# Hybrid attention block on one core: exchanged banks in the first stage, a fourth sum on another engine, probabilities turned a chunk later, values turned sooner

## The chip, the cores and the metric

The kernel runs on one core of a Trainium2 chip. The metric is the device time of one execution in microseconds (us). TensorE (PE in the profile) multiplies, VectorE (DVE), ScalarE (ACT) and GpSimd (POOL) work on elements, and SyncE (SP) issues every DMA. Each engine takes its own instructions strictly in the order written; they meet at semaphores alone.

## The reference

One layer of a streaming encoder on x of 1024 positions by 1024 channels, in fp32. One wide input projection gives queries, keys, values and gates of two mixers:

```
h = x @ w_in + b_in                      # 1024 x 5376 columns
q_a, k_a, v_a, gate_a, q_b, k_b, v_b, gate_b, mg_a, mg_b = split(h)
o_a = window_attention(rope(q_a), rope(k_a), v_a, sinks) * silu(gate_a)   # 16 chunks of 64
o_b = stick_breaking(q_b, k_b, v_b) * silu(gate_b)                        # 128-query blocks
merged = sigmoid(mg_a) * (o_a @ w_up_a) + sigmoid(mg_b) * (o_b @ w_up_b)
out = layer_norm(2**0.25 * x + merged @ w_out)
```

Window attention lets each chunk of 64 queries see its own and one neighbour chunk, with a sink logit in the softmax. Stick breaking multiplies sigmoids along the keys by a running product.

## The kernel before

**Precision.** Every fp32 operand is split into a rounded high part (ScalarE copies it) and a low part (raw minus high, a subtraction on GpSimd or VectorE). A product is three matmuls (`mma3`, lines 176 to 178).

**The projection.** Keys and values of the window mixer (tiles K_A and V_A) are done first and plainly, each in two halves of 512 positions: the keys' halves in PSUM banks 0 and 1, the values' in 2 and 3 (`first_half`). The other 40 column tiles are done as 20 pairs by a seven-product scheme after Strassen, so there are 140 products, numbered q = 7 i + pos. Each is twelve matmuls of 128x512 into bank q % 2. A product needs the low part of its weights (`part_lo`), the bank read out twice earlier (`bank_read`), and in pair 0 also a sum of quarters of x (`t_lo`). There are four sums, t = 1 to 4, made in `xr`, the buffer of raw x: VectorE makes the raw sums 1, 3 and 2 (`sum_raw`), GpSimd the fourth (`fourth_sum`), ScalarE the high parts (`sum_hi`), VectorE the low parts (`sum_lo`). For each pair the second weight tile is loaded by SP (`load_a2`), VectorE forms sums of weights (`weight_sums`), ScalarE and GpSimd split them (`part_high`, `low_part`).

**Rotation.** Rotary positions need halves of each head exchanged. For the keys ScalarE writes them exchanged into `sw` (`keys_swap`), and VectorE then rotates (`rotate_keys`: lines 1072, 1074, 1077). Products 0 and 1 wait for `k_cos` and `swapped`, since they write the banks that the keys stand in. For the queries (pairs 0 and 1) SP exchanges by four DMAs a block (`swap_halves`, line 434), and VectorE rotates (`rotate_block`: lines 1084, 1085, 1088). The first of these exchanges writes `prob`, which lies over `xr`, so SP also waits there for `t_lo` of sums 2 and 4; `load_a2(1)` stands behind it in SP's queue.

**Gates of the window mixer** (pairs 2 and 3) are put in `gate_st`, five slots of which three lie over the angles (`GATE_SLOT`). `room` keeps ScalarE from writing those slots before the queries are rotated.

**The window stage** takes from product 18 on one chunk c with each product: PE turns (transposes) the probabilities of chunk c-2 (line 1457), does the product, the scores of chunk c (line 1471), and the values' product of chunk c-3 (line 1481). VectorE does maxima and norms (lines 1196 to 1221), ScalarE the exponentials (line 924) and the copies of turned probabilities (line 914).

**The sticks**: 16 steps s, each with a big and a small unit of stick breaking between half products (`fill(s, place)`). Banks 6 and 7 serve in turn, in the order of `RING`, for turned weights "t", outputs "o" and turned values "v". Values of the next head pair are turned in steps 4, 8 and 12 (`turn_values`, line 1502; ScalarE copies them in `turned_values`, line 951). A bank may be used when the entry two back is read out: for the second half of the values that is the output of the small unit of the step before, which VectorE reads in `gated_out` (line 1258, semaphore `o_set`) only after the big unit's scans and multiplications:

```
for s in range(STEPS):
    break_sticks(s, False)
    if s > 0:
        gated_out(s - 1, True)
```

Of the kernel before, what the change touches and what calls it, by code (L numbers as in the profile page):

```python
# [51 lines left out]
BLOCKS = ((0, 0), (0, 1), (1, 1), (1, 0))  # L52
GATE_SLOT = {(0, 0): 0, (0, 1): 2, (1, 1): 4, (1, 0): 1}

# [126 lines left out]
def build(nc, xt, xn, w, bias, cos, sin, sinks, ln_g, ln_b, out):  # L181
    with ExitStack() as ctx:
# [42 lines left out]
        with ExitStack() as a1:  # L225
            qa23 = sb("qa23", [P, NCHUNK, 2, CHUNK], F32, a1)
            v_win = sb("v_win", [P, NCHUNK, P], F32, a1)
            prob = sb("prob", [P, 3, HALF], F32, a1)
            prob_t = sb("prob_t", [P, 2, HALF], F32, a1)
            oa_st = sb("oa_st", [P, 2, GROUP, P], F32, a1)  # L230
            gate_st = sb("gate_st", [P, 5, HALF], F32, a1)
        qa = (qa01, qa23)
# [92 lines left out]
        def block_at(sp, m, nh):  # L325


            if sp in Q_PAIRS:
                return qa[sp][:, 8 * nh:8 * nh + 8, m, :]
            if sp in G_PAIRS:  # L330
                return gate_st[:, GATE_SLOT[m, nh], :]
            if sp >= MG_PAIR:
                return sig_m[:, 4 * (sp % 2) + 2 * m + nh, :]
            for p in range(PAIRS):
                if sp == pair_vg(p):
                    return (o_b[p % 2] if m else v_t)[:, half(nh)]
                if sp == pair_kq(p):
                    return (qs if m else ks)[p % 2][:, half(nh)]
# [30 lines left out]
        oa_done, oa_free, oa_out = sem("oa_done"), sem("oa_free"), [sem(f"oa_out{i}") for i in range(2)]  # L369
        gate_out = [sem(f"gate_out{i}") for i in range(5)]  # L370
        z_done, keep_set, beta_set = sem("z_done"), sem("keep_set"), sem("beta_set")
# [30 lines left out]

        window_end = WINDOW_1 + NCHUNK + 2

        @block.sync
        def _(sp):
# [30 lines left out]
            def gate_store(i, m, nh):  # L437
                wait_block(sp, i, m, nh)
                at = GATE_SLOT[m, nh]
                sp.dma_start(gate_d[2 * (i - G_PAIRS[0]) + m][:, half(nh)],  # L440
                             gate_st[:, at, :]).then_inc(gate_out[at], 16)

# [79 lines left out]
            for q in range(WINDOW_1):  # L522
                after(q)
            for c in range(NCHUNK + 3):
                if c < NCHUNK + 2:
                    after(WINDOW_1 + c)
                if c >= 4 and c % 2 == 0:
                    window_store((c - 4) // 2)
            for q in range(window_end, STEP_0):
# [70 lines left out]
        def _(pool):  # L600
# [17 lines left out]

            def fourth_sum(i):


                if i == 0:
                    pool.wait_ge(x_lo_done, 2 * KT)
                pool.wait_ge(t_raw[2], i + 1)
                o = x_raw(1, 0, i)
                pool.tensor_tensor(o, o, x_raw(1, 1, i), ALU.subtract).then_inc(t_raw[4], 1)

            def cut_causal(s, small):
# [45 lines left out]
        def _(act):  # L674
# [33 lines left out]
            def keys_swap(h):  # L708


                act.wait_ge(half_done, halves_done(K_A, h))
                for q in range(4):
                    o = 32 * (q ^ 1)
                    act.activation(sw[o:o + 32, h, :], ps[32 * q:32 * q + 32, h, :], ACT.Identity,
                                   bias=b_of(K_A, 32 * q, 32 * q + 32)).then_inc(swapped, 1)

            def value_half(h):
                act.wait_ge(half_done, halves_done(V_A, h))
                act.activation(v_t[:, half(h)], ps[:, 2 + h, :], ACT.Identity, bias=b_of(V_A)).then_inc(v_read, 1)

# [16 lines left out]
            def room(i, pos):  # L737
# [6 lines left out]
                if i == G_PAIRS[0]:  # L744
                    if pos == 0:
                        act.wait_ge(t_lo[2], 2)
                    else:
                        act.wait_ge(rope_done, rope_at(Q_PAIRS[1], 3 if pos == 6 else 2) + 1)
                if i == G_PAIRS[1]:
                    act.wait_ge(gate_out[GATE_SLOT[m, nh]], 16)  # L750
                for p in range(PAIRS):
                    if i == pair_kq(p) and pos == 0:
                        if p == 0:
                            act.wait_ge(rope_done, rope_at(Q_PAIRS[1], 3) + 1)
                            act.wait_ge(gate_out[GATE_SLOT[1, 1]], 16 * len(G_PAIRS))
# [149 lines left out]
            act.wait_ge(t_lo[4], 2)  # L905
            for c in range(NCHUNK + 2):
                if c >= 2:
                    i = c - 2
                    rows = P if i < NCHUNK - 1 else CHUNK
# [33 lines left out]
            def turned_values(p):  # L943

                if p == 1:
                    for m in range(2):
                        act.wait_ge(gate_out[GATE_SLOT[m, 1 - m]], 16 * len(G_PAIRS))
                for g in range(2):
# [23 lines left out]
            for s in range(STEPS):  # L972
# [10 lines left out]
                if s % 4 == 0 and s > 0:  # L983
                    gate_b_sigmoid(s // 4)
                for q in completed(s, 2):
                    read_bank(q)
                if s % 4 == 0 and s > 0:
                    turned_values(s // 4)
                turned_blocks(s, False, (0, 1))
# [50 lines left out]
        def _(dve):  # L1040
# [5 lines left out]
            def sum_raw(t):  # L1046


                for i in range(2):
# [4 lines left out]
                    elif t == 3:  # L1054
                        dve.wait_ge(t_raw[1], i + 1)
                        dve.tensor_tensor(o, x_raw(1, 1, i), o, ALU.subtract).then_inc(t_raw[t], 1)
                    else:
                        dve.wait_ge(t_raw[3], i + 1)
                        dve.tensor_tensor(o, o, x_raw(0, 0, i), ALU.subtract).then_inc(t_raw[t], 1)

            def sum_lo(t):
# [7 lines left out]
            def rotate_keys(h):  # L1069
                k_ = ka[:, half(h)]  # L1070
                dve.wait_ge(swapped, 4 * (h + 1))
                dve.scalar_tensor_tensor(out=k_, in0=ps[:, h, :], scalar=bias_c[:, K_A:K_A + 1],
                                         in1=cos_t[:, half(h)], op0=ALU.add, op1=ALU.mult).then_inc(k_cos, 1)
# [105 lines left out]
            sum_raw(2)  # L1179
            dve.wait_ge(rope_in, 32)  # L1180
            rotate_keys(0)
            weight_sums(0, True)
            sum_lo(2)
            weight_sums(0, False)
            rotate_keys(1)
            sum_lo(3)
            sum_lo(1)
            sum_lo(4)
            for q in range(WINDOW_1):
                after(q)  # L1190
# [13 lines left out]
            dve.wait_ge(sink_set, 1)  # L1204
            for c in range(NCHUNK + 3):
                if 1 <= c <= NCHUNK:
                    prob_norm(c - 1)
                if c < NCHUNK:
# [12 lines left out]
                    dve.tensor_tensor(sm[:, 1, 0:4], sm[:, 0, 0:4], sink_c[:], ALU.add).then_inc(za_bias, 1)  # L1221
                if c < NCHUNK + 2:
# [143 lines left out]
        def _(pe):  # L1366
# [4 lines left out]
            def first_half(n, h):  # L1371


                bank = 2 + h if n == V_A else h
                for k in range(KT):
# [16 lines left out]
            def half_product(u):  # L1392
# [56 lines left out]

            for c in range(NCHUNK + 3):  # L1450
                if 2 <= c < NCHUNK + 2:
                    i = c - 2
                    keys = P if i < NCHUNK - 1 else CHUNK
# [5 lines left out]
                    last.then_inc(tp_done, 1)  # L1459
                if c < NCHUNK + 2:  # L1460
                    product(WINDOW_1 + c)
                if c < NCHUNK:
# [10 lines left out]
                    last.then_inc(za_done, 1)  # L1473
                if c >= 3:
                    i = c - 3
                    pe.wait_ge(tp_free, 4 + i + 1)
# [88 lines left out]
            for s in range(STEPS):  # L1565
# [161 lines left out]
```

## Time and profile before

| | |
|---|---|
| Median of three runs | 773.39 us (772.83, 773.39, 777.02) |
| Profiled execution | 776.86 us |
| Its span, first to last instruction | 775.1 us |
| Mean granted TensorE clock | 0.99 |
| Busy: PE, DVE, ACT, POOL | 742.1, 528.4, 404.6, 251.7 us |

The span is what the trace shows; 1.8 us of the profiled execution lie outside it. Spans of matmuls overlap, so the spacing of their starts says more than their length. "[7.26 <-issue]" behind a row is the idle time ahead of it and what ended it; "issue" means that the trace names no releaser.

### The profile page before, as it was taken

What the parts mean: (1) busy time and instruction counts of PE and PEld (TensorE: products, weight loads), DVE (VectorE), ACT (ScalarE), POOL (GpSimd) and SP (SyncE); (2) the same over time, 40 slices, a digit from 0 to 9 for tenths busy, and PEclk for the clock granted to TensorE, in tenths of its full rate; (3) what the DMA queues carried; (4) which work ended last, traced back from release to release, by engine and by line L of the source; (5) the groups of instructions that cost most, each with busy time, mean ns of one, the idle gap of its engine ahead of it and who ended that gap; (6) DMA issues with size and microseconds to landing.
All of it is one profiled execution on the core that took longest, in us unless ns stands there. A gap on an engine that the chain in (4) does not pass through costs nothing.

```text
span 775.1 us, 10717 instructions
## 1 busy us (share of the span) xinstructions
PE 742.1 (96%) x3944; PEld 580.3 (75%) x3944; DVE 528.4 (68%) x684; ACT 404.6 (52%) x760; POOL 251.7 (32%) x225
## 2 busy tenths in 40 slices
PE   8789889999999999999999999999999999999996
PEld 7567666766677777777777777888887888888884
DVE  6987887883579768786977876344457566770644
ACT  6833356664766567676657765555565121150221
POOL 0544423223332123223212323445443221200692
PEclk9989999999999999999999999999999999999998
DMA  9114432222010020102001222355554444341351
GB/s 312 69 34 103 91 100 82 84 67 69 28 55 29 28 82 1 55 1 82 28 28 59 79 69 69 125 183 194 189 193 132 178 164 158 114 164 54 114 199 68
DMA packets 41204, 76.22 MB, mean 98 GB/s; under 512 B 12224, under 2 KB 16320, under 8 KB 41152
## 3 DMA queue, kind: packets, MB, share of 16 engines
q1 hardware_dynamic: 41152, 75.54, 29.9%
q8 instruction: 32, 0.52, 0.3%
q14 instruction: 20, 0.16, 0.1%
HBM read 55.07 MB, written 18.35 MB: 95 GB/s over the span
## 4 chain that ended last, share of the span: by engine, by line
PE 69%; DVE 16%; ACT 5%; DMA 3%; issue 3%; SPq 2%; POOL 1%; ACTq 0%; DVEq 0%; POOLq 0%
PE ps L176 19%; PE ps L178 18%; PE ps L177 18%; PE ps L1519 5%; PE ps L1548 5%; PE ps L1535 4%; DVE small L1218 2%; ACT prob L924 2%; DMA raw<-in_w 2%; DVE prob L1201 1%; DVE small L1214 1%; DVE t_ops L1066 1%; SPq L434 1%; DMA xr<-in_xt 1%; DVE raw L1108 1%
## 5 line engine op out<-in xcount | busy, mean ns | idle before, releaser
L176 PE MATMUL ps<-x_hi,w_hi 128*128 128x512 f32 x448 | 182.9, 408 | 8.8 <-issue 7.3
L178 PE MATMUL ps<-x_hi,w_lo 128*128 128x512 f32 x448 | 175.9, 393 | 0.0
L177 PE MATMUL ps<-x_lo,w_hi 128*128 128x512 f32 x448 | 175.5, 392 | 0.0
L616 POOL TENSOR_TENSOR w_lo<-raw,w_hi 128x512 fp32r<-128x512 f32 x72 | 100.9, 1412 | 100.2 <-ACT w_hi L706 100.0
L176 PE MATMUL ps<-t_ops,w_hi 128*128 128x512 f32 x272 | 110.3, 406 | 5.8 <-ACT gate_st L798 4.0
L176 PEld LDWEIGHTS ps<-x_hi,w_hi 128*128 128x128 f32 x448 | 84.7, 189 | 36.1 <-issue 14.9
L178 PE MATMUL ps<-t_ops,w_lo 128*128 128x512 f32 x272 | 107.0, 393 | 0.0
L177 PE MATMUL ps<-t_ops,w_hi 128*128 128x512 f32 x272 | 106.8, 393 | 0.0
L178 PEld LDWEIGHTS ps<-x_hi,w_lo 128*128 128x128 f32 x448 | 84.6, 189 | 18.3
L177 PEld LDWEIGHTS ps<-x_lo,w_hi 128*128 128x128 f32 x448 | 84.9, 190 | 15.3
L1241 DVE TENSOR_TENSOR_SCAN keep_big<-keep_big 128x1023 f32<-128x1023 f32 (+3 forms) x32 | 63.4, 1981 | 31.1 <-POOL keep_big L636 29.1
L706 ACT ACTIVATE w_hi<-raw 128x512 fp32r<-128x512 f32 x120 | 73.5, 632 | 6.7 <-DVE raw L1114 3.4
L636 POOL TENSOR_SCALAR_AFFINE_SELECT keep_big<-keep_big 128x128 f32<-128x128 f32 x32 | 29.5, 923 | 139.6 <-ACT keep_big L963 139.6
L176 PEld LDWEIGHTS ps<-t_ops,w_hi 128*128 128x128 f32 x272 | 51.5, 189 | 21.3 <-issue 8.9
L178 PEld LDWEIGHTS ps<-t_ops,w_lo 128*128 128x128 f32 x272 | 51.5, 189 | 11.3
L177 PEld LDWEIGHTS ps<-t_ops,w_hi 128*128 128x128 f32 x272 | 51.5, 189 | 9.7
L793 ACT ACTIVATE tmp<-ps 128x512 f32<-128x512 f32 x60 | 36.1, 601 | 42.1 <-PE ps L178 42.1
L1099 DVE TENSOR_TENSOR sig_m<-sig_m,tmp 128x512 f32<-128x512 f32 x32 | 24.4, 784 | 40.5 <-ACT tmp L793 40.5
L963 ACT ACTIVATE keep_big<-ps 128x1023 f32<-128x1023 f32 (+3 forms) x32 | 25.9, 862 | 38.9 <-PE ps L1519 38.9
L1519 PE MATMUL ps<-ks,qs 64*128 64x512 f32 (+3 forms) x192 | 39.6, 517 | 0.9 <-ACT beta_big L965 0.9
L1332 DVE SCALAR_TENSOR_TENSOR o_t<-raw,ps 128x512 f32<-128x512 f32 x16 | 10.9, 683 | 43.0 <-PE ps L178 34.6
L1121 DVE TENSOR_TENSOR w_lo<-raw,w_hi 128x512 fp32r<-128x512 f32 x48 | 34.7, 738 | 8.0 <-ACT w_hi L706 8.0
(170 smaller groups left out, 1311.3 us busy)
## 6 DMA issues: line engine op xcount, KB each, us to landing
raw<-in_w SPq DMA_DIRECT2D x28, 512.0 KB, 3.9
raw<-in_w SPq DMA_DIRECT2D x44, 256.0 KB, 3.0
sig_d<-sig_m SPq DMA_DIRECT2D x32, 256.0 KB, 3.3
sig_m<-sig_d SPq DMA_DIRECT2D x16, 512.0 KB, 4.2
xr<-in_xt SPq DMA_DIRECT2D x16, 256.0 KB, 6.8
raw<-in_xn SPq DMA_DIRECT2D x8, 512.0 KB, 3.7
out<-o_t SPq DMA_DIRECT2D x16, 256.0 KB, 2.3
o_t<-o_d SPq DMA_DIRECT2D x7, 512.0 KB, 4.9
```

What stands on the lines that cost most here:

```text
L176: pe.matmul(out, w_hi, x_hi, start=first, stop=False, skip_group_check=goes_on)
L177: pe.matmul(out, w_hi, x_lo, start=False, stop=False, skip_group_check=goes_on)
L178: return pe.matmul(out, w_lo, x_hi, start=False, stop=last, skip_group_check=goes_on)
L616: pool.tensor_tensor(ring_slot(w_lo, q), part_of(q), ring_slot(w_hi, q).bitcast(F32), ALU.subtract).then_inc(part_lo, 1)
L636: pool.affine_select(out=kp_d, in_=kp_d, compare_op=ALU.is_gt, fill=1.0, base=0, pattern=[[1, n]], channel_multiplier=-1).then_inc(keep_cu ...
L706: act.activation(ring_slot(w_hi, q), part_of(q), ACT.Copy).then_inc(part_hi, 1)
L793: act.activation(tmp[:, e % 2, :], bank, ACT.Copy).then_inc(bank_read, 1)
L1121: dve.tensor_tensor(ring_slot(w_lo, q), part_of(q), ring_slot(w_hi, q).bitcast(F32), ALU.subtract).then_inc(part_lo, 1)
L1241: dve.tensor_tensor_scan(stick, stick, stick, 1.0, ALU.mult, ALU.bypass).then_inc(scanned, 1)
L1519: last = pe.matmul(ps[:, 2 + 2 * h + at // HALF, 0:m], qs[p % 2][r, P * tb:P * (tb + 1)], ks[p % 2][r, P * tb + at:P * tb + at + m], start ...
L1535: last = pe.transpose(bank[:, at:at + P], bt[:, h, P * b_:P * (b_ + 1)], ident[:])
L1548: last = pe.matmul(bank[r, 0:P], v_n[p % 2][:, tb + b_, r], w_t[:, turned_block(small, b_), h, :], start=b_ == 0, stop=b_ == nb - 1)
```

## The change

Six edits:

1. Keys and values exchange banks: values in 0 and 1, keys in 2 and 3. Products 0 and 1 now wait for ScalarE's copies of the values (`v_read`).
2. The fourth sum goes from GpSimd to VectorE, behind the other three.
3. VectorE rotates the keys only after all sums but behind the first addition of a block (`after(0)`, `after(1)`).
4. `gate_st` has two slots; blocks (0,1) and (1,1) go to `sw`. ScalarE waits there for the keys' rotation instead of the queries'.
5. PE turns the probabilities of chunk c-3 instead of c-2, and everything behind it in the chunk loop comes one chunk later.
6. `turn_values` on PE stands ahead of `fill(s, 2)`, and `turned_values` on ScalarE ahead of `read_bank` of that place.

```diff
-GATE_SLOT = {(0, 0): 0, (0, 1): 2, (1, 1): 4, (1, 0): 1}
+GATE_SLOT = {(0, 0): 0, (1, 0): 1, (0, 1): 2, (1, 1): 3}
...
-                return gate_st[:, GATE_SLOT[m, nh], :]
+                slot = GATE_SLOT[m, nh]
+                return gate_st[:, slot, :] if slot < 2 else sw[:, slot - 2, :]
...
-            fourth_sum(0)
-            low_part(0)
-            low_part(1)
-            fourth_sum(1)
-            low_part(2)
+            for q in range(3):
+                low_part(q)
...
+                    elif pos == 6:
+                        act.wait_ge(rope_done, rope_at(Q_PAIRS[1], 3) + 1)
                     else:
-                        act.wait_ge(rope_done, rope_at(Q_PAIRS[1], 3 if pos == 6 else 2) + 1)
+                        act.wait_ge(rope_done, 2)
...
+            value_half(0)
             keys_swap(0)
-            value_half(0)
             sum_hi(1)
             sum_hi(3)
             part_high(0)
             part_high(1)
             sum_hi(2)
             keys_swap(1)
+            value_half(1)
             part_high(2)
-            value_half(1)
             sum_hi(4)
...
                     if q < 2:
-                        pe.wait_ge(k_cos, q + 1)
-                        pe.wait_ge(swapped, 4 * (q + 1))
+                        pe.wait_ge(v_read, q + 1)
...
-            for c in range(NCHUNK + 3):
-                if 2 <= c < NCHUNK + 2:
-                    i = c - 2
+            for c in range(NCHUNK + 4):
+                if 3 <= c < NCHUNK + 3:
+                    i = c - 3
...
-                if c >= 3:
-                    i = c - 3
+                if c >= 4:
+                    i = c - 4
...
                 scores(s, True)
-                fill(s, 2)
                 if s % 4 == 0 and s > 0:
                     turn_values(s // 4)
+                fill(s, 2)
                 turn(s, False, (0, 1))
```

**VectorE, from the fourth raw sum to the first exchange of a block of queries.** xr is raw x and its sums, t_ops and x_lo take the low parts, raw and w_x are weights, ka and sw the keys, qa the queries; in brackets stand the semaphores waited for. Before:

```order
L1072 SCALAR_TENSOR_TENSOR ka<-ps,bias_c,angles 128x512 [waits swapped,rope_in]
L1074 TENSOR_TENSOR sw<-sw,angles 128x512
L1077 TENSOR_TENSOR ka<-ka,sw 128x512 [waits sin_mul,k_cos]
L1108 TENSOR_TENSOR raw<-raw 128x512 [waits part_lo,a2_in]
L1110 TENSOR_TENSOR w_x<-raw 128x512 [waits w_sum]
L1066 TENSOR_TENSOR t_ops<-xr,t_ops 128x1024 [waits t_hi2] x2
L1114 TENSOR_TENSOR raw<-raw,w_x 128x512 [waits w_sum,part_lo]
L1115 TENSOR_TENSOR raw<-raw 128x512
L1072 SCALAR_TENSOR_TENSOR ka<-ps,bias_c,angles 128x512 [waits swapped]
...
L1066 TENSOR_TENSOR x_lo<-xr,x_hi 128x2x512 [waits t_hi4] x2
L1099 TENSOR_TENSOR qa<-qa,tmp 128x8x64 [waits bank_read] x2
```

Of the change (its line numbers are a few lower):

```order
L1052 TENSOR_TENSOR xr<-xr 128x2x512 [waits t_raw2] x2
L1101 TENSOR_TENSOR raw<-raw 128x512 [waits part_lo,a2_in]
L1103 TENSOR_TENSOR w_x<-raw 128x512 [waits w_sum]
L1059 TENSOR_TENSOR t_ops<-xr,t_ops 128x1024 [waits t_hi2] x2
L1107 TENSOR_TENSOR raw<-raw,w_x 128x512 [waits w_sum,part_lo]
L1108 TENSOR_TENSOR raw<-raw 128x512
L1059 TENSOR_TENSOR t_ops<-xr,t_ops 128x1024 [waits t_hi3] x2
L1059 TENSOR_TENSOR t_ops<-xr,t_ops 128x1024 [waits t_hi1] x2
L1092 TENSOR_TENSOR qa<-qa,tmp 128x8x64 [waits bank_read]
L1059 TENSOR_TENSOR x_lo<-xr,x_hi 128x2x512 [waits t_hi4] x2
L1065 SCALAR_TENSOR_TENSOR ka<-ps,bias_c,angles 128x512 [waits swapped,rope_in]
```

The six operations of the keys have moved behind the low part of the fourth sum (x_lo), and two operations of the fourth raw sum have come in ahead.

**PE, in step 4 of the sticks, from the small unit's scores to the turning of the big unit's weights.** ks and qs are keys and queries, v_t the values to be turned, beta_big the weights. Before:

```order
L1519 MATMUL ps<-ks,qs 128x128 [waits beta_set]
...
L176 MATMUL ps<-t_ops,w_hi 128x512 [waits bank_read,part_lo]
...
L1502 MATMUL ps<-ident,v_t 128x128 [waits turned_out,block_sum]
L1502 MATMUL ps<-ident,v_t 128x128 x3
L1502 MATMUL ps<-ident,v_t 128x128 [waits o_set]
L1502 MATMUL ps<-ident,v_t 128x128 x3
L1535 MATMUL ps<-ident,beta_big 128x128 [waits turned_out,w_ready]
```

Of the change:

```order
L1515 MATMUL ps<-ks,qs 128x128 [waits beta_set]
L1515 MATMUL ps<-ks,qs 128x128
L1498 MATMUL ps<-ident,v_t 128x128 [waits turned_out,block_sum]
L1498 MATMUL ps<-ident,v_t 128x128 x3
L1498 MATMUL ps<-ident,v_t 128x128 [waits o_set]
L1498 MATMUL ps<-ident,v_t 128x128 x3
L176 MATMUL ps<-x_hi,w_hi 128x512
...
L1531 MATMUL ps<-ident,beta_big 128x128 [waits turned_out,w_ready]
```

The eight transposes now stand ahead of the twelve matmuls of two half products, and the wait for `o_set` with them.

## Rows read from the trace of the kernel before

**Rows 1.** The page, part 1: TensorE's busy time, share of the span, instructions.

```profile
PE 742.1 (96%) x3944; PEld 580.3 (75%) x3944; DVE 528.4 (68%) x684; ACT 404.6 (52%) x760; POOL 251.7 (32%) x225
```

**Rows 2.** Waits of PE: us in total, times, longest.

```profile
PE ps L176 <- issue: 7.3, 1, 7.3
PE ps L1457 <- DVE prob L1201: 4.9, 8, 1.6
PE ps L176 <- ACT gate_st L798: 4.0, 1, 4.0
...
PE ps L1535 <- ACT v_n L951: 1.1, 3, 0.4
```

**Rows 3.** Timeline of PE, products 0 and 1: start us, us, what.

```profile
31.65 0.50 PE L176 MATMUL ps<-x_hi,w_hi 128*128 128x512 f32 x1 [0.46 <-POOL w_lo L616]
...
34.27 0.39 PE L178 MATMUL ps<-x_hi,w_lo 128*128 128x512 f32 x1
41.92 0.77 PE L176 MATMUL ps<-x_hi,w_hi 128*128 128x512 f32 x1 [7.26 <-issue]
```

**Rows 4.** Windows, 42 to 45 us: busy of each engine, then PEclk, DMA.

```profile
42.00:45.00 3.00, 3.00 (x7) 2.40 (x8) 2.90 (x3) 0.00 (x0) 2.26 (x2) 0.50 0.30 87
```

**Rows 5.** Timeline of DVE, 27 to 56 us.

```profile
27.54 0.74 DVE L1072 SCALAR_TENSOR_TENSOR ka<-ps,bias_c,angles 128x512 f32<-128x512 f32 x1
...
44.73 4.62 DVE L1066 TENSOR_TENSOR t_ops<-xr,t_ops 128x1024 fp32r<-128x1024 f32 x4
49.27 4.55 DVE L1066 TENSOR_TENSOR x_lo<-xr,x_hi 128x1024 fp32r<-128x1024 f32 x2
53.74 2.40 DVE L1099 TENSOR_TENSOR qa<-qa,tmp 128x512 f32<-128x512 f32 x2
```

**Rows 6.** Timeline of POOL, the same stretch.

```profile
26.64 3.26 POOL L626 TENSOR_TENSOR xr<-xr 128x1024 f32<-128x1024 f32 x1 [25.11 <-DVE xr L1059]
...
48.22 2.27 POOL L616 TENSOR_TENSOR w_lo<-raw,w_hi 128x512 fp32r<-128x512 f32 x1 [3.97 <-ACT w_hi L706]
```

**Rows 7.** Timeline of ACT: the keys' second exchange.

```profile
30.26 2.80 ACT L714 ACTIVATE sw<-ps,bias_c 32x512 f32<-32x512 f32 x4
```

**Rows 8.** Timeline of SP: the first exchange of queries, the weights behind it.

```profile
55.56 2.70 SPq L434 DMA_DIRECT2D prob<-qa  x4
58.30 0.60 SPq L420 DMA_DIRECT2D raw<-in_w  x1
```

**Rows 9.** Timelines of DVE and PE: who needs those weights.

```profile
63.32 0.69 DVE L1108 TENSOR_TENSOR raw<-raw 128x512 f32<-128x512 f32 x1 [1.40 <-DMA raw<-in_w]
```

```profile
67.12 0.50 PE L176 MATMUL ps<-t_ops,w_hi 128*128 128x512 f32 x1 [0.62 <-POOL w_lo L616]
```

**Rows 10.** Timelines of PE and DVE ahead of the window stage.

```profile
97.40 0.60 PE L176 MATMUL ps<-t_ops,w_hi 128*128 128x512 f32 x1 [3.99 <-ACT gate_st L798]
...
101.91 0.72 PE L1471 MATMUL ps<-ka,qa 64*128 64x128 f32 x8
```

```profile
98.39 1.59 DVE L1088 TENSOR_TENSOR qa<-qa,prob_t 128x512 f32<-128x512 f32 x1
```

**Rows 11.** Timelines of ACT and PE in the window stage.

```profile
121.38 0.61 ACT L914 ACTIVATE prob_t<-ps 128x512 f32<-128x512 f32 x1
```

```profile
122.69 0.65 PE L1457 MATMUL ps<-ident,prob 128*128 128x128 f32 x4 [1.23 <-DVE prob L1201]
...
179.23 0.65 PE L1481 MATMUL ps<-prob_t,v_win 128*64 128x256 f32 x4 [0.18 <-DVE oa_st L1229]
```

**Rows 12.** Timeline of PE and DVE in step 4 of the sticks.

```profile
277.84 0.50 PE L176 MATMUL ps<-x_hi,w_hi 128*128 128x512 f32 x1
...
279.85 0.28 DVE L1258 TENSOR_TENSOR o_b<-o_b,ps 128x128 f32<-128x128 f32 x1
...
280.75 1.04 PE L1502 MATMUL ps<-ident,v_t 128*128 128x128 f32 x8
...
282.21 1.12 PE L1535 MATMUL ps<-ident,beta_big 128*128 128x128 f32 x8 [0.42 <-ACT v_n L951]
```

More of the change, by code:

```diff
@@ L369, in build @@
         oa_done, oa_free, oa_out = sem("oa_done"), sem("oa_free"), [sem(f"oa_out{i}") for i in range(2)]
-        gate_out = [sem(f"gate_out{i}") for i in range(5)]
+        gate_out = [sem(f"gate_out{i}") for i in range(4)]
         z_done, keep_set, beta_set = sem("z_done"), sem("keep_set"), sem("beta_set")
@@ L400, in rope_at @@
             return 2 + 4 * i + b
-        window_end = WINDOW_1 + NCHUNK + 2
+        window_end = WINDOW_1 + NCHUNK + 3
         @block.sync
@@ L523, in _ @@
                 after(q)
-            for c in range(NCHUNK + 3):
-                if c < NCHUNK + 2:
+            for c in range(NCHUNK + 4):
+                if c < NCHUNK + 3:
                     after(WINDOW_1 + c)
-                if c >= 4 and c % 2 == 0:
-                    window_store((c - 4) // 2)
+                if c >= 5 and c % 2 == 1:
+                    window_store((c - 5) // 2)
             for q in range(window_end, STEP_0):
@@ L718, in value_half @@
                 act.wait_ge(half_done, halves_done(V_A, h))
-                act.activation(v_t[:, half(h)], ps[:, 2 + h, :], ACT.Identity, bias=b_of(V_A)).then_inc(v_read, 1)
+                act.activation(v_t[:, half(h)], ps[:, h, :], ACT.Identity, bias=b_of(V_A)).then_inc(v_read, 1)
             def first_weights_hi(n, h):
@@ L754, in room @@
                             act.wait_ge(rope_done, rope_at(Q_PAIRS[1], 3) + 1)
-                            act.wait_ge(gate_out[GATE_SLOT[1, 1]], 16 * len(G_PAIRS))
+                            for m in range(2):
+                                act.wait_ge(gate_out[GATE_SLOT[m, 1]], 16 * len(G_PAIRS))
                         else:
@@ L905, in _ @@
             act.wait_ge(t_lo[4], 2)
-            for c in range(NCHUNK + 2):
-                if c >= 2:
-                    i = c - 2
+            for c in range(NCHUNK + 3):
+                if c >= 3:
+                    i = c - 3
                     rows = P if i < NCHUNK - 1 else CHUNK
@@ L945, in turned_values @@
                 if p == 1:
-                    for m in range(2):
-                        act.wait_ge(gate_out[GATE_SLOT[m, 1 - m]], 16 * len(G_PAIRS))
+                    act.wait_ge(gate_out[GATE_SLOT[1, 0]], 16 * len(G_PAIRS))
                 for g in range(2):
@@ L984, in _ @@
                     gate_b_sigmoid(s // 4)
+                    turned_values(s // 4)
                 for q in completed(s, 2):
                     read_bank(q)
-                if s % 4 == 0 and s > 0:
-                    turned_values(s // 4)
                 turned_blocks(s, False, (0, 1))
@@ L1179, in _ @@
             sum_raw(2)
-            dve.wait_ge(rope_in, 32)
-            rotate_keys(0)
+            sum_raw(4)
             weight_sums(0, True)
@@ L1184, in _ @@
             weight_sums(0, False)
-            rotate_keys(1)
             sum_lo(3)
             sum_lo(1)
+            after(0)
+            after(1)
             sum_lo(4)
-            for q in range(WINDOW_1):
+            dve.wait_ge(rope_in, 32)
+            rotate_keys(0)
+            after(2)
+            rotate_keys(1)
+            for q in range(3, WINDOW_1):
                 after(q)
@@ L1204, in _ @@
             dve.wait_ge(sink_set, 1)
-            for c in range(NCHUNK + 3):
+            for c in range(NCHUNK + 4):
                 if 1 <= c <= NCHUNK:
@@ L1371, in first_half @@
             def first_half(n, h):
-                bank = 2 + h if n == V_A else h
+                bank = 2 + h if n == K_A else h
                 for k in range(KT):
@@ L1448, in _ @@
                     last.then_inc(tp_done, 1)
-            for c in range(NCHUNK + 3):
-                if 2 <= c < NCHUNK + 2:
-                    i = c - 2
+            for c in range(NCHUNK + 4):
+                if 3 <= c < NCHUNK + 3:
+                    i = c - 3
                     keys = P if i < NCHUNK - 1 else CHUNK
@@ L1459, in _ @@
                     last.then_inc(tp_done, 1)
-                if c < NCHUNK + 2:
+                if c < NCHUNK + 3:
                     product(WINDOW_1 + c)
@@ L1473, in _ @@
                     last.then_inc(za_done, 1)
-                if c >= 3:
-                    i = c - 3
+                if c >= 4:
+                    i = c - 4
                     pe.wait_ge(tp_free, 4 + i + 1)
```

21 lines of the change are left out of this document (9 added, 12 removed).

## The prediction

> **What bounds the kernel now.** I read the page first: TensorE is busy 742.1 of 775.1 us [rows 1], so whatever delays it counts in full, and the question is where it idles. The list of its waits gives four entries that the change aims at: 7.3 us once, 4.0 us once, 4.9 us in eight pieces at the turning of probabilities, 1.1 us in three at the turning of values [rows 2]. Then I read the timeline of each place.
>
> The 7.3 us lie between product 0, whose last matmul starts at 34.27, and product 1 at 41.92 [rows 3]. The trace says "issue", but product 1 waits for `k_cos`, whose second operation (line 1072) ends on VectorE when PE starts. The row 42 to 45 us has a granted clock of 0.50, the 1.2 GHz level [rows 4]; the first ten matmuls start 0.43 us apart instead of 0.23, which is 2.0 us more. So the place costs up to 0.5 + 7.3 + 2.0 = 9.8 us. The 3.99 us ahead of 97.40 [rows 10] are ScalarE kept in `room` until the queries are rotated; nine matmuls at the low clock follow, 1.8 us.
>
> What limits the stretch between them? Not PE. The chain of waits runs there through SP, the DMAs and VectorE: four exchange DMAs from 55.56, the weights behind them in SP's queue at 58.30 [rows 8], landed for VectorE at 63.32, and through ScalarE and GpSimd to PE at 67.12, which had idled 0.62 us for it [rows 9]. It goes on in that way to the last rotation, which ends at 98.39 + 1.59 = 99.98; the scores of chunk 0 at 101.91 need it [rows 10].
>
> **Edits 1 to 3, the head.** PE itself: values replace keys in ScalarE's list. Its first copy waits for the values' half, so the list runs some 0.35 us later; the keys' second exchange, 30.26 + 2.80 before [rows 7], ends at 33.4, the second copy of values at 34.1. Product 1 starts there instead of 41.92: 7.8 us, and without the slow clock. But product 6 needs the low part of the fourth sum, and, what matters more, SP needs it before the exchange at 55.56. I therefore sum VectorE's list.
>
> Prices first. Four operations on 1024 elements take 4.62 us, 1.14 each, while GpSimd rests; two of the same kind take 4.55 when GpSimd has two subtractions beside them (one is the 2.27 us row at 48.22) [rows 5, 6]. So each of GpSimd's operations costs VectorE 1.14 us: they exclude each other. Of the two additions in 2.40 us one such piece leaves 0.62 for an operation on 512 elements [rows 5].
>
> The Trainium skill, page "SBUF — State Buffer", section "SBUF: two separate sides", says the same of a VectorE operation with two SBUF inputs against a GpSimd operation that reads SBUF: an exclusive lock for the whole instruction, not shared bandwidth. If they did not exclude each other the list below would be 10 us shorter; this case's rows side with the page.
>
> The new list starts where line 1072 started, 27.54 [rows 5]: two of the fourth sum, eight low parts (ten at 1.14 = 11.4), four weight sums and one addition (five at 0.62 = 3.1), 14.5 us together. GpSimd now has nothing but low parts of weights in that time, and since PE runs earlier they come sooner: parts 0 to 8 are all ready before the end (part 8 after product 4, which ends near 46), in turn with VectorE, nine by 1.14 = 10.3 us. `t_lo` of sum 4 is complete at 27.5 + 14.5 + 10.3 = 52.3. Before, SP's exchange was released by the first addition at 55.5. The advance is 3.2 us; with ten of GpSimd's in it 2.1, with seven 5.5.
>
> All that follows on SP, DMA and VectorE keeps its distances: exchange at 52.4, weights issued at 55.1, product 9 able to start at 67.12 - 3.2 = 63.9. PE would be there near 59.8 (product 6 waits until 52.5 for the fourth sum, ends at 53.9; two products at 2.73, four transposes). So a wait of about 4 us takes the place of the one of 7.3. The keys' rotation, moved behind, takes some 4 us from 52.3 and lies under the DMAs, which end at 56.6 and 60.1; without that cover it would stand in the chain.
>
> **Edit 4, the gates.** The 3.99 us and the 1.8 us of slow clock disappear at that place. But the scores of chunk 0 wait for the same rotation, one product later. It now ends at 99.98 - 3.2 = 96.8. PE, with a slow clock after the gap at product 9, gets there near 95.0 and waits 2 us; without the slow clock it waits 4. Either way the scores start at 96.85 against 101.91: **5.1 us gained** by edits 1 to 4 together, of which 1.9 is PE's former lateness against the rotation. Bounds: 2.1 + 1.9 = 4.0 and 5.5 + 1.9 = 7.4.
>
> **Edit 5, probabilities a chunk later.** It looks like 4.9 us. But from 107 to 175 the chain of waits runs through VectorE and ScalarE alone: norm, maximum, bias, four exponentials, norm again, which takes 4.3 to 5.9 us a chunk, while PE's own work for one is 4.63 where it waits for nothing (transposes at 116.83, the next ones could go at 121.46; the rows of this stretch of the timeline are too many to stand here). Those operations don't move. With one chunk more between, PE's transposes are no longer bound by the norm, but by the bank: ScalarE copies the turned probabilities of c-4 only behind the exponentials of c-2. That copy starts at 121.38 and ends at 121.99, where the norm let PE go at 122.69 [rows 11]. PE runs 0.6 us closer to the loop, once, not per chunk. At the end it waits for the copy of an output by VectorE (0.18 us at 179.23 [rows 11]), which stays where it is. I take **0.3 us gained**, between 0.6 and a loss of 1.0 (if PE, which is ahead by a chunk at first and then waits some 2.5 us in one piece, falls to the low clock there, or at the scores).
>
> **Edit 6, values sooner.** This loses. In step 4 PE starts the two half products at 277.84, the values at 280.75, and the big unit's weights at 282.21, after 0.42 us for ScalarE's copy [rows 12]. Moved ahead, the first four transposes can run at 277.84, but the second four wait for `o_set`, and VectorE reads that output at 279.85 to 280.13 [rows 12], behind scans and multiplications that hang on the big unit's scores, already past. So PE idles from 278.36 to 280.18, turns to 280.70, does its half products (2.91 us, 277.84 to 280.75) until 283.61, and only then the weights: 1.4 us later than before, the 0.42 included. The half products were the cover of that wait. Steps 8 and 12 have the same rows 68.5 and 136.9 us later; **4.2 us lost** in all, 3.7 to 4.7. PE has hardly a wait left in those steps that could absorb it.
>
> **Sum.** -5.1 - 0.3 + 4.2 = -1.2 us: the profiled 776.86 becomes 775.7, the span 773.9. The profiled execution lies 3.5 us above the median of the three runs, so I take the difference from the median: 773.39 - 1.2 = **772.2 us**. The likeliest case's own range is 773.39 - 7.4 - 0.6 + 3.7 = 769.1 to 773.39 - 4.0 + 1.0 + 4.7 = 775.1. A measurement of this kernel tells about 0.5%, 3.9 us, from no change: one of the three runs is 3.6 above the others.
>
> **The rivals.**
> (a) The chain through SP is no limit, and PE's own earliness survives (chance 0.10). It needs VectorE's list to end by about 46, so hardly any exclusion. PE would reach product 9 at 59.8, 7.3 us early, and with 3.99 + 1.8 more at the gates gain 13.1: 773.39 - 13.1 - 0.3 + 4.2 = 764.2. Against it speak rows 5 and 6.
> (b) The values' move costs nothing and removes its 1.1 us (0.08): if VectorE read the output before PE asks. 773.39 - 5.1 - 0.3 - 1.1 = 766.9. Against it: 279.85 lies 1.5 us behind the point at which PE would ask [rows 12].
> (c) Slower than before: VectorE's list is not earlier (0.12). It carries the fourth sum and nine subtractions in turn; if the exclusion costs more, or SP's exchange is released at 55.5 as before, only the 1.9 us remain: 773.39 - 1.9 + 4.2 = 775.7. The point from which it decides is an end of the list at 53.5: there the gain of the head equals edit 6.
> (d) The clock. The Trainium skill, page "TensorE: Matmul & The Clock Gate", section "HAM oscillation — how this bites in real kernels", says that gaps in the matmuls bring the clock back to its low level each time; rows show it after 7.26 and 3.99 us of idleness [rows 3, 4, 10] and not after 1.23 [rows 11]. The change makes gaps of about 4 us ahead of product 9, 2 ahead of the scores and 2.5 in the window stage. Only one behind the scores would count, about 2 us: 774.2 (0.10).
>
> The rest, 0.60, is the forecast. From these: faster than before by over 0.5% 0.28 ((a), (b) and a tenth of the forecast's lower edge with the scatter of runs), within 0.5% 0.62, slower 0.10. The range has to hold (b) and (c) with the scatter: 766.8 to 776.8.
>
> **What would show it.** Right: in the changed trace PE starts product 1 near 34; SP's first exchange is issued near 52.4; PE waits some 4 us for GpSimd's part ahead of product 9 near 64; the scores start near 97; the turning of probabilities waits for ScalarE's copy; in steps 4, 8 and 12 PE idles 1.8 us ahead of the second half of the values, for line 1258's successor. Wrong: an exchange issued before 48 or after 55, no wait ahead of product 9, a chunk of the window stage in under 4.7 us, or no wait in the middle of the values.

## The result, and the profile after

The change takes 778.28 us (median of 20 runs, 774.52 to 780.73), the kernel before, run beside it, 775.15 us (20 runs, 772.22 to 777.60). The ratio is 1.0049, 95% interval 1.0037 to 1.0061: 3.8 us slower by the ratio, 3.1 by the two medians. The interval leaves out 1, so the change is slower, though just inside the 0.5% that the forecast called no change. Forecast were 1.2 us faster, and 778.28 lies above the range's 776.8. Ratios here and below leave out runs far off the others of their kernel: one of e9's nine, at 919.33 us, and one of the 21 of before beside e9 to e11, at 2107.13 us.

The profiled execution of the change took 776.80 us, 1.5 us less than its median. That of before took 776.86 us, 1.7 us more than its median. By these two the change looks like -0.06 us.

The page of the changed kernel, first part:

```profile
PE 740.8 (96%) x3944; PEld 578.8 (75%) x3944; DVE 528.1 (68%) x686; ACT 404.9 (52%) x760; POOL 251.1 (32%) x223
```

TensorE's work is the same [rows 1]. Its list of waits (us in total, times, longest):

```profile
PE ps L1498 <- DVE o_b L1255: 5.0, 3, 1.7
PE ps L176 <- POOL w_lo L617: 4.5, 1, 4.5
PE ps L1453 <- ACT prob_t L906: 3.7, 5, 1.5
PE ps L1477 <- DVE oa_st L1226: 2.8, 5, 1.3
PE ps L1467 <- DVE qa L1081: 2.4, 1, 2.4
PE ps L176 <- DVE x_lo L1059: 1.6, 2, 1.1
```

Against [rows 2] the 7.3 and the 4.0 us are gone, but 4.5 wait for a weight's low part, 2.4 for the last rotation, 1.6 for the fourth sum. The turning of probabilities now waits for ScalarE's copy. And 5.0 us in three pieces are new: the turning of values in steps 4, 8 and 12.

The head, timeline of PE:

```profile
33.81 0.47 PE L176 MATMUL ps<-x_hi,w_hi 128*128 128x512 f32 x1 [0.37 <-ACT v_t L708]
...
49.38 0.47 PE L176 MATMUL ps<-x_hi,w_hi 128*128 128x512 f32 x1 [1.11 <-DVE x_lo L1059]
...
51.51 0.50 PE L176 MATMUL ps<-x_hi,w_hi 128*128 128x512 f32 x1 [0.53 <-DVE x_lo L1059]
...
63.58 0.80 PE L176 MATMUL ps<-t_ops,w_hi 128*128 128x512 f32 x1 [4.53 <-POOL w_lo L617]
...
97.49 0.71 PE L1467 MATMUL ps<-ka,qa 64*128 64x128 f32 x8 [2.39 <-DVE qa L1081]
```

Timelines of DVE, POOL and SP in the same stretch:

```profile
37.39 7.91 DVE L1059 TENSOR_TENSOR t_ops<-xr,t_ops 128x1024 fp32r<-128x1024 f32 x4
45.22 1.78 DVE L1092 TENSOR_TENSOR qa<-qa,tmp 128x512 f32<-128x512 f32 x1
46.93 4.53 DVE L1059 TENSOR_TENSOR x_lo<-xr,x_hi 128x1024 fp32r<-128x1024 f32 x2
51.38 0.74 DVE L1065 SCALAR_TENSOR_TENSOR ka<-ps,bias_c,angles 128x512 f32<-128x512 f32 x1
```

```profile
37.61 12.77 POOL L617 TENSOR_TENSOR w_lo<-raw,w_hi 128x512 fp32r<-128x512 f32 x6 [1.29 <-ACT w_hi L695]
```

```profile
51.56 2.70 SPq L435 DMA_DIRECT2D prob<-qa  x4
54.31 0.60 SPq L421 DMA_DIRECT2D raw<-in_w  x1
```

The prediction's chain can be read off here. Product 1 starts at 33.81. VectorE's list ends at 51.46, SP's exchange goes out at 51.56, product 9 starts at 63.58 after 4.53 us of idleness, the scores at 97.49 (101.91 in [rows 10]). From 37.39 on VectorE's and GpSimd's operations go in turn: VectorE's four take 7.91 us where they took 4.62 [rows 5], GpSimd's six take 2.1 each. Behind the 4.53 us the granted clock is 0.50 from 64 to 69 us; that costs nothing, since PE then still waits 2.39 us for the scores' rotation.

Step 4, timelines of PE and DVE:

```profile
273.73 0.49 PE L1515 MATMUL ps<-ks,qs 64*128 64x128 f32 x4
274.15 0.66 PE L1498 MATMUL ps<-ident,v_t 128*128 128x128 f32 x4
276.48 0.66 PE L1498 MATMUL ps<-ident,v_t 128*128 128x128 f32 x4 [1.67 <-DVE o_b L1255]
276.89 0.47 PE L176 MATMUL ps<-x_hi,w_hi 128*128 128x512 f32 x1
...
279.74 1.03 PE L1531 MATMUL ps<-ident,beta_big 128*128 128x128 f32 x8
```

```profile
276.15 0.27 DVE L1255 TENSOR_TENSOR o_b<-o_b,ps 128x128 f32<-128x128 f32 x1
```

PE turns the first four blocks at 274.15 and then stands 1.67 us until VectorE has read the output. From the first four blocks to the big unit's weights it is 5.59 us here; in [rows 12], from the half products that stood there (277.84) to the weights (282.21), 4.37. So 1.22 us are lost at each of three places.

Lastly the stretches. From the first values' turning behind the window stage to the end of the span it is 581.8 us before (775.1 - 193.34) and 585.5 in the change (775.1 - 189.65): 3.7 us, all of it edit 6 (e1 below, which differs in edit 6 alone, has 581.8 again). Between scores and values lie 91.43 us before and 92.16 in the change: 0.7 lost where edit 5 was to gain.

### The profile page after: what moved, and what is told of

The parts are those of the page before. It is cut to its first block, busy times and chain, and to the rows that moved or that the text cites. A ratio compares the mean times of both kernels' runs of the same rounds, so it can differ in the third digit from the quotient of the medians.

```text
span 775.1 us, 10717 instructions
## 1 busy us (share of the span) xinstructions
PE 740.8 (96%) x3944; PEld 578.8 (75%) x3944; DVE 528.1 (68%) x686; ACT 404.9 (52%) x760; POOL 251.1 (32%) x223
## 4 chain that ended last, share of the span: by engine, by line
PE 69%; DVE 17%; ACT 5%; issue 4%; DMA 3%; POOL 2%; SPq 1%; DVEq 0%; ACTq 0%; POOLq 0%
PE ps L176 19%; PE ps L178 18%; PE ps L177 18%; PE ps L1515 5%; PE ps L1544 4%; PE ps L1531 4%; ACT prob L916 2%; DVE small L1215 2%; DMA prob<-qa 1%; DVE prob L1198 1%; DVE keep_big L1238 1%; DVE small L1211 1%; DMA raw<-in_w 1%; DVE beta_big L1245 1%; DVE qa L1078 1%
## 5 line engine op out<-in xcount | busy, mean ns | idle before, releaser
L617 POOL TENSOR_TENSOR w_lo<-raw,w_hi 128x512 fp32r<-128x512 f32 x72 | 104.3, 1462 | 118.8 <-ACT w_hi L695 118.7
L617 POOL TENSOR_TENSOR w_lo<-w_x,w_hi 128x512 fp32r<-128x512 f32 x12 | 17.5, 1458 | 75.5 <-ACT w_hi L695 75.5
```

Source lines behind the costliest of these rows:

```text
L617: pool.tensor_tensor(ring_slot(w_lo, q), part_of(q), ring_slot(w_hi, q).bitcast(F32), ALU.subtract).then_inc(part_lo, 1)
```

## The experiments

The first four ask which part carries the loss, and how much of the difference belongs to the execution that was traced. The next four price the edits: 1 to 4 together, then 5 alone, 4 alone, and 1 to 3, which were not separated further. The last four test the cause in edit 6 and look for a better version. "Before" is always the kernel before, run beside the experiment on the same chip.

**e1: the change without edit 6.**

```
                 betas(s, True)
                 if s % 4 == 0 and s > 0:
                     gate_b_sigmoid(s // 4)
-                    turned_values(s // 4)
                 for q in completed(s, 2):
                     read_bank(q)
+                if s % 4 == 0 and s > 0:
+                    turned_values(s // 4)
...
                 scores(s, True)
+                fill(s, 2)
                 if s % 4 == 0 and s > 0:
                     turn_values(s // 4)
-                fill(s, 2)
```

> The change without edit 6 (values turned where they were before). Theory: edit 6 costs 3.6 us, 1.2 us at each of three places, so this kernel is 3.6 us faster than the change and within 1.5 us of the kernel before. Rival (the loss lies in the head or the window stage): it stays 3 to 4 us slower than before.

Measured: 773.31 us (12 runs), ratio 0.9978 [0.9965, 0.9992]; the stretch from values to the end is back at 581.8 us. Against the change's 1.0049 edit 6 costs 0.7%, some 5.5 us. The place is right, but the waits explain only 3.7 of it.

**e2: before with edit 6** (the same lines in the kernel before).

> The kernel before with edit 6 alone. Theory: 3.6 us slower than before, ratio 1.0047, with PE idle 1.7 us ahead of the second half of the values in steps 4, 8 and 12. Rival: under 1.5 us slower.

Measured: 779.14 us (7 runs), 1.0068 [1.0039, 1.0098]. So 5.3 us by the ratio, without any of the other edits. Its windows (us, busy of PE, PEld, DVE, ACT and POOL, PEclk, DMA) from 338 and from 405, over the turnings of steps 8 and 12:

```profile
338.00:355.00 17.00, 15.08 (x85) 11.22 (x84) 13.68 (x17) 10.13 (x18) 5.07 (x6) 0.90 0.19 63
405.00:425.00 20.00, 18.08 (x119) 13.56 (x119) 17.71 (x22) 12.80 (x23) 5.07 (x6) 1.00 0.14 43
```

The granted clock fell at step 8, not at step 12. This was the first sign of what the waits leave unexplained.

**e3 and e4: before and the change once more, unedited.**

> The kernel before once more, for a second trace. If the profiled execution of before (1.7 us above the median) was an odd one, this trace shows a shorter span, and where: the theory is a low clock or none after the 4 us gap ahead of product 18, 1.8 us. Ratio to before 1.000.

> The changed kernel once more, for a second trace. Its profiled execution was 1.5 us below its median at the highest clock of all its runs (0.994 against 0.989 to 0.991). Theory: a usual execution has one more stretch at the low clock, after a gap that the change made (product 6, product 9, the scores, or the window stage), worth 1.5 to 2 us. Ratio to before 1.0049.

Measured: before again 775.25 us, 0.9998 [0.9980, 1.0017], and its trace has the gap of 4.0 us of [rows 10] and the low clock behind it again. The first profile of before was therefore no odd one at this place. Its span is 774.1 us, 1.0 less, all of it ahead of the scores (100.89 against 101.91). The change again: 778.87 us, 1.0055 [1.0036, 1.0075], and its trace differs from the change's first, timeline of PE at the scores and at step 8:

```profile
96.33 0.94 PE L1467 MATMUL ps<-ka,qa 64*128 64x128 f32 x8 [3.60 <-DVE qa L1081]
97.20 0.79 PE L176 MATMUL ps<-t_ops,w_hi 128*128 128x512 f32 x1
97.80 0.63 PE L177 MATMUL ps<-t_ops,w_hi 128*128 128x512 f32 x1
...
343.25 0.65 PE L1498 MATMUL ps<-ident,v_t 128*128 128x128 f32 x4
345.58 0.89 PE L1498 MATMUL ps<-ident,v_t 128*128 128x128 f32 x4 [1.68 <-DVE o_b L1255]
346.12 0.77 PE L176 MATMUL ps<-x_hi,w_hi 128*128 128x512 f32 x1
346.70 0.63 PE L177 MATMUL ps<-x_lo,w_hi 128*128 128x512 f32 x1
...
350.44 1.03 PE L1531 MATMUL ps<-ident,beta_big 128*128 128x128 f32 x8
```

Here PE waits 2.83 us ahead of product 9, not 4.53, and 3.60 at the scores, not 2.39. And the big unit's weights come 7.19 us after the first four blocks, where step 4 of the change's first trace has 5.59: 1.6 us more, with the same wait of 1.7. The expectation had the low clock among four places, of which the scores were one; steps 8 and 12 were not among them. Matmuls take 0.63 us instead of 0.40, the level of 1.2 GHz. The windows of this trace, as above:

```profile
338.00:355.00 17.00, 15.08 (x88) 11.98 (x86) 12.38 (x14) 11.85 (x22) 4.77 (x5) 0.90 0.20 63
405.00:425.00 20.00, 18.08 (x111) 13.73 (x107) 15.05 (x19) 12.91 (x23) 5.07 (x6) 0.91 0.16 53
```

The change's first trace has 1.00 in both:

```profile
338.00:355.00 17.00, 15.09 (x109) 12.21 (x109) 13.08 (x15) 12.47 (x22) 5.06 (x6) 1.00 0.19 63
405.00:425.00 20.00, 18.09 (x126) 13.95 (x124) 14.59 (x19) 14.04 (x24) 5.07 (x6) 1.00 0.18 53
```

The stretch to the end follows: 585.5 us with none of these drops (first trace), 587.0 with one (e2), 588.6 with two (e4), some 1.6 us each.

**e5: edits 1 to 4** (the change without edits 5 and 6: the lines of e1 and these, with the loops of the engines one chunk shorter).

```
-                if c >= 3:
-                    i = c - 3
+                if c >= 2:
+                    i = c - 2
```

> Edits 1 to 4 alone (5 and 6 undone). Theory: edit 5 costs 0.9 us in the window stage (92.2 to 92.8 us from the first scores to the first values, against 91.4), so this kernel is 2.6 us faster than before (ratio 0.9966), and the stretch takes 91.4 us again. Rival, as forecast: edit 5 gains 0.3 us, so this kernel is no faster than the one with edit 5 (ratio 0.998 or above).

Measured: 771.83 us (770.70 to 772.84), 0.9968 [0.9954, 0.9983], 2.5 us faster. Its span of 770.3 is 4.8 us under the 775.1 of before's first trace, close to the 5.1 forecast against that execution. Both numbers are true: before's runs beside it (35) lie in three groups, around 772.4, 774.1 and 776.0 us, and both traces of before come from the upper one; e5's runs have one group.

**e6: before with edit 5.**

> The kernel before with edit 5 alone. Theory: the window stage is bound by VectorE and ScalarE, the waits of PE move from the norm to ScalarE's copy and to VectorE's copy of outputs; 0.9 us slower, ratio 1.001, stretch of 92.3 us. Rival by the list of waits: 4.9 us faster.

Measured: 776.07 us, 1.0020 [1.0002, 1.0038]: 1.5 us slower. Its waits in the window stage:

```profile
PE ps L1457 <- ACT prob_t L914: 4.1, 5, 1.9
...
PE ps L1481 <- DVE oa_st L1229: 2.8, 5, 1.3
```

The 4.9 us that the norm cost have become 4.1 for the bank, and the wait for VectorE's copies of outputs has grown from 0.8 to 2.8 us: 1.2 us more together; from scores to values it takes 92.48 us (91.43 before). The rival, 4.9 us gained, has fallen.

**e7: before with edit 4.**

```
-GATE_SLOT = {(0, 0): 0, (0, 1): 2, (1, 1): 4, (1, 0): 1}
+GATE_SLOT = {(0, 0): 0, (1, 0): 1, (0, 1): 2, (1, 1): 3}
...
+                    elif pos == 6:
+                        act.wait_ge(rope_done, rope_at(Q_PAIRS[1], 3) + 1)
                     else:
-                        act.wait_ge(rope_done, rope_at(Q_PAIRS[1], 3 if pos == 6 else 2) + 1)
+                        act.wait_ge(rope_done, 2)
```

> The kernel before with edit 4 alone (gates in the swap buffer). Theory: the 4.0 us wait for the gates moves one product on, to the scores of chunk 0, which start 1.9 us earlier than before at the end of the rotation; a low clock behind the gap takes about 1 us of it back: 0.5 to 1.9 us faster. Rival by the list of waits: 5.8 us faster (4.0 and 1.8 of low clock).

Measured: 774.08 us, 0.9989 [0.9974, 1.0003]. The 4.0 us ahead of 97.40 are gone, and 3.25 of them stand a product later, timeline of PE:

```profile
98.68 1.23 PE L1474 MATMUL ps<-ka,qa 64*128 64x128 f32 x8 [3.25 <-DVE qa L1091]
99.84 0.79 PE L176 MATMUL ps<-t_ops,w_hi 128*128 128x512 f32 x1
```

The low clock has moved with the wait. The rival, 5.8 us gained, has fallen.

**e8: before with edits 1 to 3** (the diff's parts on banks, the fourth sum and VectorE's list).

> Edits 1 to 3 alone (banks, fourth sum, keys rotated later; gates as before). Theory: the chain from the low part of the fourth sum through SP and the DMAs is 3 to 4 us earlier, and the wait for the gates, which ends with the same rotation, moves with it: product 18 starts at 93 to 94.5 instead of 97.4, the result is 2.5 to 3.5 us faster. Rival (PE's own earliness survives): 8 us or more.

Measured: 772.09 us, 0.9975 [0.9958, 0.9992], 1.9 us faster, less than the 2.5 to 3.5 expected; the scores start at 96.72. PE waits 4.6 us ahead of product 9. Its runs lie in two groups, around 771.5 and 773.7 us. Product 18 starts at 93.79, after 1.9 us for the gates, as expected. The rival, eight or more for the 7.3 us taken away, has fallen. With e7's 0.9989 this makes 0.9964, e5's 0.9968 within the scatter.

**e9: edits 1 to 4, and only the first half of the values ahead.** Four blocks are turned ahead of `fill(s, 2)`, which covers the wait, and four behind it; ScalarE's two copies in `turned_values` are parted in the same way. Shown against e5:

```
                 scores(s, True)
+                if s % 4 == 0 and s > 0:
+                    turn_values(s // 4, (0,))
                 fill(s, 2)
                 if s % 4 == 0 and s > 0:
-                    turn_values(s // 4)
+                    turn_values(s // 4, (1,))
```

> Edits 1 to 4, and of the values only the first half turned sooner (ahead of the half products), the second half where it was. Theory: the loss of edit 6 is the wait of the second half for the output bank; without it the first half's copy is hidden and the waits of 0.42 us shrink: 0 to 1 us faster than edits 1 to 4 alone, ratio to before 0.996. Rival (the transposes' early place itself costs, or splits the clock): slower than edits 1 to 4.

Measured: 771.46 us, 0.9954 [0.9933, 0.9976]. No wait for `o_b` is left in its trace, timeline of PE:

```profile
273.41 0.66 PE L1500 MATMUL ps<-ident,v_t 128*128 128x128 f32 x4
...
276.66 0.60 PE L1500 MATMUL ps<-ident,v_t 128*128 128x128 f32 x4
```

So it was the loss of the cover that cost, not the early turning itself: against the change's 1.0049 both the wait and edit 5 are gone, against e5's 0.9968 nothing is lost. That it beats e5 isn't shown: the intervals overlap.

**e10: edits 1 to 4, the next weights sent ahead of the exchange** and their sum formed between the two rotations of keys.

```
-                if pos == 2 and i + 1 < N_PAIRS:
+                if pos == (1 if i == 0 else 2) and i + 1 < N_PAIRS:
...
+            weight_sums(1, True)
```

> Edits 1 to 4, with the second weights of pair 1 loaded ahead of the first exchange in SP's queue and summed between the two rotations of keys. Theory: the wait of 3 to 4.5 us ahead of product 9 goes, since it hangs on SP's order alone; but the scores still wait for the rotation, which comes only 1.2 us earlier, and PE's wait moves there (5 us and more, with a low clock behind it): 0 to 1.5 us faster than edits 1 to 4. Rival (PE's earliness is worth itself): 3 us or more faster than edits 1 to 4.

Measured: 770.89 us, 0.9950 [0.9929, 0.9971]. The waits, which were 4.2 and 2.5 in e5, are

```profile
PE ps L1469 <- DVE qa L1082: 3.9, 1, 3.9
...
PE ps L176 <- POOL w_lo L617: 2.4, 1, 2.4
```

Of what product 9 no longer waits (1.8 us) the scores wait 1.4: they hang on the last rotation. They start 1.5 us sooner (96.17 against 97.69), but a low clock follows the longer wait and takes that back: from scores to values it takes 92.43 us against 90.97 in e5.

**e11: the change, with its idle stretch filled.** Twelve transposes of the unit matrix, which nobody reads, stand ahead of the second four blocks.

```
                 for g in range(2):
+                    if g and p:
+                        for _ in range(12):
+                            pe.transpose(ps[:, 5, 0:P], ident[:], ident[:])
```

> The whole change with 12 transposes of the identity in an unused bank ahead of the second half of the values in steps 4, 8 and 12, in the 1.7 us in which PE idles. They compute nothing that is used. Theory: of the 5.3 us that edit 6 costs, 3.65 are its wait and the rest is the low clock that follows the idle stretch in some executions; with the stretch filled the granted clock is 1.00 at all three places in the profile and the ratio falls from 1.005 to 1.0025. Rival (the clock has no part in it): 1.005 or more.

Measured: 776.93 us (774.50 to 777.88), 1.0025 [1.0008, 1.0043], and step 4 in its timeline of PE:

```profile
274.95 0.66 PE L1501 MATMUL ps<-ident,v_t 128*128 128x128 f32 x4
275.44 1.47 PE L1498 MATMUL ps<-ident 128*128 128x128 f32 x12
277.28 0.66 PE L1501 MATMUL ps<-ident,v_t 128*128 128x128 f32 x4 [0.37 <-DVE o_b L1255]
```

The second four blocks come 2.33 us after the first, as in the change: nothing is gained in the wait. The clock is 1.00 over steps 4, 8 and 12 in its trace, and the ratio is 0.0024 under the change's in the first comparison (0.0030 under e4's): 1.9 to 2.3 us. Useless work made the kernel faster, as far as this can be told: the intervals of e11 and of the change just overlap (1.0043 and 1.0037), so the size is loose. Against e1, the same kernel without edit 6, e11 is still 0.0047 or 3.6 us slower, with intervals well apart: the price of the three waits alone, three times 1.22 us.

**e12: e9 and e10 together.**

> Edits 1 to 4 with both: the weights ahead of the exchange, and the first half of the values sooner. Theory: the two gains add, 1.4 and 1.1 us over edits 1 to 4 alone, ratio to before 0.994 (0.992 to 0.996). Rival: no better than either alone, 0.995.

Measured: 771.37 us (7 runs, 770.10 to 771.59), before 775.39, 0.9943 [0.9921, 0.9965], the lowest ratio of all. It beats before and the change; that it beats e5, e9 or e10 isn't shown.

## Why the prediction was wrong, step by step

Measured are 778.28 us, 6.1 above the forecast 772.2. Of these 1.8 are the base: the forecast started from 773.39, the median of three runs, where 20 give 775.15; from that base the same range would have ended at 778.6 and held the result. The rest is the change itself, forecast 1.2 us faster and measured 3.8 slower by the ratio, and there three steps of the sum failed: a difference within one trace was taken off the median (edits 1 to 4, 5.1 forecast, 2.5 measured), edit 5 had the wrong sign (0.3 gained against 0.8 to 1.5 lost), and edit 6 was priced by its wait alone (4.2 against 5.5).

**Edits 1 to 3, the head: right.** "`t_lo` of sum 4 is complete at … 52.3" (measured 51.46), "exchange at 52.4" (51.56), "product 9 able to start at … 63.9" (63.58), "a wait of about 4 us takes the place of the one of 7.3" (4.53). The reading that the 7.3 us hid a chain through VectorE, SP and the DMAs held; rival (a) has fallen with the 4.53 us, rival (c) with the exchange at 51.56. One assumption, that all behind the exchange "keeps its distances", holds only roughly: from SP's exchange to product 9 pass 12.0 us in the change's first trace, 10.3 in its second (51.88 to 62.20) and 11.6 before. The mutual exclusion of VectorE and GpSimd, on which the list's length hung, shows in both engines' rows.

**Edit 4: right.** The scores started at 97.49 and 96.33 in two traces, forecast 96.85; e7 shows that the wait only moves to "the same rotation, one product later". By the ratio e7 gains 0.9 us, and its interval holds 1, so a gain of edit 4 alone isn't shown.

**The difference from one trace, taken off the median: this step failed, and it is the largest miss (2.6 us).** The forecast took a difference worked out in one execution, "5.1 us gained", off the median of the runs. Between traces it is 4.8 us (e5), but by the ratio only 2.5. Before's runs form groups, and against the lowest (772.4) edits 1 to 4 gain next to nothing, against the upper one (776.0), from which the trace came, 4.2. What differs inside before between the groups wasn't traced, since both traces come from the upper one, and stays open. Their mean clocks are about 0.993, 0.988 and 0.990, so it isn't the clock alone.

**Edit 5: wrong sign.** "PE runs 0.6 us closer to the loop" held at the bank, but "At the end it waits for the copy of an output by VectorE …, which stays where it is" failed. The outputs are made a chunk later, too, and the wait for their copies grew from 0.8 to 2.8 us. They are five waits instead of two, the first already at 139.78 us and not at the stage's end; why VectorE comes to these copies late wasn't followed. Measured: 1.5 us lost (e6, interval 0.2 to 2.9), and 0.8 us between e5 and e1 (0.9968 and 0.9978, whose intervals overlap), forecast 0.3 gained. It lies at or just beyond the loss of 1.0 that was kept as a bound.

**Edit 6: mechanism right, price too small.** PE idles ahead of the second four blocks in exactly the three places, 1.67 us for a forecast 1.8, and loses 1.22 us at each for a forecast 1.4: 3.7 for 4.2. But it costs 5.3 to 5.5 us (e2; e1 against the change). The step that failed stands under rival (d): "Only one behind the scores would count". In the head that held: the low clock behind product 9 cost nothing. But the prediction looked for low clocks behind gaps of 2 to 4 us alone, and named 1.23 us as one behind which none follows. The idle stretches of 1.67 us in steps 4, 8 and 12 were not in that list. In two of three traces with edit 6 the clock fell behind one or two of them, 1.6 us each (e2, e4), and with the stretches filled (e11) some 2 us come back. That the drops cost this is shown by e4 and e2 for single executions; for the runs e11 supports it, with intervals that just overlap.

The mean granted clock, which is on record for every run, closes the sum. It is 0.9908 over the change's 32 runs (the first 20 and e4's 12), 0.9934 over the 12 without edit 6 (e1) and 0.9940 over the 12 with the stretch filled (e11). Edit 6 lowers it by 0.0026, of 777 us 2.0 us of TensorE's time, an estimate and rather too high, since a low clock over an idle stretch is counted and costs nothing. With 3.7 for the waits that makes 5.7 against 5.5 measured, and at 1.6 us a drop it is a little over one drop in each execution. In e2 the mean clock is only 0.0011 under before's (0.9891 over seven runs, 0.9902 over 30), 0.9 us; the sum, 4.6, lies within e2's interval of 3.0 to 7.6. Why the same idle stretch is followed by a drop in one execution and not in the next stays open.

**The sum.** By the ratios: -2.5 (e5) + 0.8 (e1 against e5) + 5.5 (the change against e1) = +3.8 us, as measured. Of the 5.0 us between forecast and ratio, 2.6 come from the size of edits 1 to 4, 1.1 from edit 5, 1.3 from edit 6.

The rule on gaps from the Trainium skill, page "TensorE: Matmul & The Clock Gate", section "HAM oscillation — how this bites in real kernels", was weighed and given a chance of 0.10. Its case is a kernel that waits long for a DMA in every round of a loop, and pays a low clock each time. The traces agree with it at the scores (behind 3.6 us in e4, 3.25 in e7, 3.9 in e10). It doesn't speak of stretches as short as 1.7 us, and there the traces show a low clock behind three of nine. What the forecast lacked is a price for every new idle stretch of the change, and not for the longest alone.

## What to carry to other kernels

Before work is moved ahead of its neighbour, read what its second half waits for: the neighbour may be the cover, and moving only the half that is free (e9) keeps it. Price each new idle stretch of TensorE twice, once for the wait and once for a low clock behind it, also where the stretch is under 2 us. And a difference worked out in one traced execution belongs to that execution: if the runs of a kernel lie in groups, see which group the trace is from before taking it off the median, and don't take three runs for the median.

## What the hardware did that I had not expected

The clock fell behind an idle stretch of only 1.68 us between two groups of four small transposes (e4, e2), with seven or eight large matmuls at 0.6 us behind it instead of 0.4, and did not fall behind the same stretch of 1.67 us in the change's first trace: same program, same wait, another outcome. In [rows 11] 1.23 us had no such effect.

The wait at the scores behaves more evenly: 2.39 and 2.46 us of idleness (the change, e5) left the clock at its upper level, 3.25 to 3.9 us (e7, e4, e10) did not. So the length of the idle stretch alone doesn't decide: 1.7 us among small matmuls brought the clock down three times in nine, 2.4 us behind large ones didn't.

VectorE and GpSimd did not only exclude each other but alternated: four of VectorE's operations in 7.91 us, six of GpSimd's in 12.77, 2.0 and 2.1 us for each, where VectorE alone needs 1.14. In the change's trace GpSimd's start at 37.61, 39.72, 41.95 and 44.18, VectorE's second to fourth at 38.52, 40.76 and 42.99, each in the middle of one of the other's.
